# Moving two more column tiles of a layer's input from TensorE transposes to VectorE squares and a DRAM exchange, with small weights loaded later

## The reference, cut to what matters

```python
for l in range(DEPTH):
    (r_q, r_k, r_v, a_cq, a_ckv, a_kpe, l_x, l_v, l_o, l_i, l_f, c_q, z) = split(x @ w_in[l])
    ret  = head_norm(retention(r_q, r_k, r_v))
    mla  = latent_attention(rmsnorm(a_cq) @ w_uq[l], rmsnorm(a_ckv) @ w_ukv[l], a_kpe)
    mls  = head_norm(mlstm(conv(l_x) @ ml_w_q[l], conv(l_x) @ ml_w_k[l], l_v, l_i, l_f) * sigmoid(l_o)) + skip
    memo = cross_attention(c_q, mem @ w_mem_kv[l])
    y    = (concat(ret, mla, mls, memo) * silu(z)) @ w_out[l]
    x    = layernorm(ALPHA * x + y) * ln_g[l] + ln_b[l]
```

## Time and profile before

| what | value |
|---|---|
| median of 3 runs | 887.83 us (887.66 to 887.92) |
| the profiled execution | 888.09 us, of which the span of its instructions 886.3 us |
| PE busy | 880.4 us, 99% of the span |
| PEld (weight loads) | 756.2 us, 85% |
| DVE busy | 665.6 us, 75% |
| ACT busy | 488.4 us, 55% |
| TensorE clock granted | 0.999 of full speed |
| DMA | 200.33 MB, mean 226 GB/s |

### The profile page before, as it was taken

How to read it: one execution, slowest core, us unless ns; L and a number is a source line. 1 busy time by engine, 2 the same in 40 slices (tenths; PEclk the granted TensorE clock), 3 DMA queues, 4 the chain that set the end, 5 groups by cost and what they waited for, 6 DMA issues and landing times.

```text
span 886.3 us, 13162 instructions
## 1 busy us (share of the span) xinstructions
PE 880.4 (99%) x4508; PEld 756.2 (85%) x4508; DVE 665.6 (75%) x1326; ACT 488.4 (55%) x914; POOL 18.0 (2%) x18
## 2 busy tenths in 40 slices
PE   9999999999999999999999999999999999999997
PEld 8888998888888888888888889888888888888896
DVE  6869697878695677766679787968777878786765
ACT  6655776545455346544477556755355453565641
POOL 0000000000000000000000000000000001000001
PEclk9999999999999999999999999999999999999999
DMA  9796487547769677566577866884485865867832
GB/s 358 294 324 205 135 263 257 185 141 222 225 222 312 216 245 256 199 198 194 194 237 232 297 252 176 267 261 167 144 266 163 278 228 161 289 218 258 320 89 95
DMA packets 72402, 200.33 MB, mean 226 GB/s; under 512 B 9608, under 2 KB 24208, under 8 KB 71696
## 3 DMA queue, kind: packets, MB, share of 16 engines
q1 hardware_dynamic: 71760, 198.44, 67.9%
q10 hardware_dynamic: 576, 1.05, 0.4%
HBM read 183.43 MB, written 16.00 MB: 225 GB/s over the span
## 4 chain that ended last, share of the span: by engine, by line
PE 98%; issue 1%; DMA 0%; ACT 0%; POOL 0%; DVE 0%; POOLq 0%; ACTq 0%; DVEq 0%
PE acc L1357 24%; PE acc L1358 24%; PE acc L1361 24%; PE acc L1372 10%; PE acc L1378 5%; PE work L1138 1%; PE work L1137 1%; PE work L1136 1%; PE work L1262 1%; DMA B<-in_mem_t 0%; PE work L1285 0%; PE work L1274 0%; PE work L1194 0%; PE work L1188 0%; PE acc L1398 0%
## 5 line engine op out<-in xcount | busy, mean ns | idle before, releaser
L1095 ACT ACTIVATE hi<-raw 128x512 fp32r<-128x512 f32 (+2 forms) x607 | 356.3, 604 | 300.3 <-PE acc L1361 242.5
L1446 DVE TENSOR_TENSOR lo<-raw,hi 128x512 fp32r<-128x512 f32 (+2 forms) x607 | 387.2, 655 | 176.7 <-ACT hi L1095 167.8
L1357 PE MATMUL acc<-hi,xx 128*128 128x512 f32 (+2 forms) x768 | 285.5, 374 | 0.0
L1358 PE MATMUL acc<-hi,xx 128*128 128x512 f32 (+2 forms) x768 | 283.6, 372 | 0.0
L1361 PE MATMUL acc<-lo,xx 128*128 128x512 f32 (+2 forms) x768 | 223.0, 372 | 0.0
L1357 PEld LDWEIGHTS acc<-hi,xx 128*128 128x128 f32 x768 | 144.6, 188 | 23.6
L1358 PEld LDWEIGHTS acc<-hi,xx 128*128 128x128 f32 x768 | 144.6, 188 | 23.6
L1361 PEld LDWEIGHTS acc<-lo,xx 128*128 128x128 f32 x768 | 140.4, 188 | 24.6
L1372 PE MATMUL acc<-xx,hi 128*128 128x512 f32 x384 | 96.0, 392 | 0.0
L1372 PEld LDWEIGHTS acc<-xx,hi 128*128 128x128 f32 x384 | 69.3, 189 | 12.6
L1378 PEld LDWEIGHTS acc<-xx,lo 128*128 128x128 f32 x384 | 52.4, 190 | 3.7
(11 more groups left out here) (355 smaller groups left out, 960.1 us busy)
## 6 DMA issues: line engine op xcount, KB each, us to landing
raw<-in_w SPq DMA_DIRECT2D x263, 512.0 KB, 4.3
B<-turn SPq DMA_DIRECT2D x80, 128.0 KB, 4.6
raw<-in_w SPq DMA_DIRECT2D x26, 256.0 KB, 2.7
turn<-B SPq DMA_DIRECT2D x12, 512.0 KB, 5.8
raw<-in_w SPq DMA_DIRECT2D x16, 328.0 KB, 3.3
turn<-Y SPq DMA_DIRECT2D x8, 512.0 KB, 5.6
Y<-in_wuq SPq DMA_DIRECT2D x2, 1152.0 KB, 8.3
Y<-in_x_t SPq DMA_DIRECT2D x4, 512.0 KB, 8.7
```

Source lines behind the costliest of these rows:

```text
L1095: act.activation(place(l, t, hi), raw[:, s, (t % 2) * w:(t % 2 + 1) * w], ACT.Copy)\
L1357: pe.matmul(o, ah[:, q], hi[:, s, 0:w], start=k == 0, stop=False, skip_group_check=name == "memv")
L1358: pe.matmul(o, al[:, q], hi[:, s, 0:w], start=False, stop=False, skip_group_check=name == "memv")
L1446: dve.tensor_tensor(place(l, t, lo), raw[:, s, (t % 2) * w:(t % 2 + 1) * w], place(l, t, hi).bitcast(F32), ALU.subtract).then_inc(lo_done. ...
```

## The change

Layer 2's columns 512 to 1023 (`xT` 2 and 3) go the way of columns 1024 to 2047: one more pair of DVE square transposes, one more store and four more loads. The normalised blocks come in the order 1, 2, 3, 0 of column blocks, the squares behind DVE tiles 10, 12, 14, the stores at couples 10, 11, 12, the loads at couples 13, 14, 15, each waiting for its own store. The third square takes B6, so `lw` is loaded at couple 33. `wuq` is loaded at couple 36, and split behind tiles 77, 108 and 118 on ACT and 79, 109 and 120 on DVE, in both layers. `wukv` stays where it was.

```diff
-for _j in range(4):
+for _j in range(2):
     _put(LATER_PE, 18 + _j // 2 * 4, "xT", _j)
...
-    _put(LATER_ACT, 8 + _j, "normalise", (4, 5, 6, 7, 0, 1, 2, 3)[_j])
+    _put(LATER_ACT, 8 + _j, "normalise", (2, 3, 4, 5, 6, 7, 0, 1)[_j])
...
-_put(LATER_DVE, 11, "square_x", 2)
-_put(LATER_DVE, 13, "square_x", 3)
+for _cb in range(1, 4):
+    _put(LATER_DVE, 8 + 2 * _cb, "square_x", _cb)
...
 for _k in range(3):
-    _put(ACT_AT, 45 + _k, "wuq", _k)
-    _put(DVE_AT, 46 + _k, "lo", "wuq", _k)
+    _put(ACT_AT, (77, 108, 118)[_k], "wuq", _k)
+    _put(DVE_AT, (79, 109, 120)[_k], "lo", "wuq", _k)
...
-        x_squares, x_turned = ([B[i][:, 0:1024] for i in pair] for pair in ((4, 5), (2, 0)))
+        x_squares, x_turned = ([B[i][:, 0:1024] for i in pair] for pair in ((4, 5, 6), (7, 2, 0)))
...
-                    if m == 20:
+                    if m == 33:
                         sp.dma_start(B[6][:, 0:1024], a["lw"][l:l + 1, :].rearrange("o (p n) -> p (o n)", p=P))\
...
                         sp.dma_start(Y[:, 0:1024], a["wukv"][l:l + 1, :].rearrange("o (p n) -> p (o n)", p=P))\
                           .then_inc(mlaw_in.sem, 16)
+                    if m == 36:
                         sp.dma_start(Y[:, 1024:3328], a["wuq"][l:l + 1, :].rearrange("o (p n) -> p (o n)", p=P))\
...
-                    if l and m in (10, 11):
+                    if l and m in (10, 11, 12):
                         sp.wait_ge(x_squared.sem, m - 9)
-                        sp.dma_start(a["x_turn"][m - 10], x_squares[m - 10]).then_inc(x_turn_out.sem, 16)
-                    if l and m in (14, 15):
-                        sp.wait_ge(x_turn_out.sem, 2 * 16)
+                        sp.dma_start(a["x_turn"][m - 10], x_squares[m - 10]).then_inc(x_turn_out[m - 10].sem, 16)
+                    if l and m in (13, 14, 15):
+                        sp.wait_ge(x_turn_out[m - 13].sem, 16)
                         for b in range(4):
...
-                    if j < 4:
+                    if j < 2:
                         wait_job(act, l, ("xT", j))
                     else:
                         act.wait_ge(xT_in[j // 2].sem, 16 + 4 * 16)
...
-                    pe.wait_ge(normed.sem, 2 * (j // 2) + 6)
+                    pe.wait_ge(normed.sem, 2 * (j // 2) + 8)
```

More of the change, by code:

```diff
@@ L458, in build_trunk @@
         early = [Br[i][:, :].rearrange("p (a k t) -> p a k t", a=2, k=2) for i in (1, 2, 3, 0)]
-        x_squares, x_turned = ([B[i][:, 0:1024] for i in pair] for pair in ((4, 5), (2, 0)))
+        x_squares, x_turned = ([B[i][:, 0:1024] for i in pair] for pair in ((4, 5, 6), (7, 2, 0)))
         def x_block(j, n):
-            return x_turned[j // 2 - 2].rearrange("p (a i j r) -> p j i a r", a=4, i=NT, j=4)[:, j % 2 * 2 + n]
+            return x_turned[j // 2 - 1].rearrange("p (a i j r) -> p j i a r", a=4, i=NT, j=4)[:, j % 2 * 2 + n]
         def y_part(part, j):
@@ L546, in build_trunk @@
         scaled, copied = signal("scaled", 0), signal("copied", 0)
-        x_squared, x_turn_out = signal("x_squared", 0), signal("x_turn_out", 0, step=16)
+        x_squared, x_turn_out = signal("x_squared", 0), [signal(f"x_turn_out{cb}", 0, step=16) for cb in (1, 2, 3)]
         stored = signal("stored", 0, step=16)
@@ L751, in _ @@
                           .then_inc(mrow_in.sem, 16)
-                    if l and m in (10, 11):
+                    if l and m in (10, 11, 12):
                         sp.wait_ge(x_squared.sem, m - 9)
-                        sp.dma_start(a["x_turn"][m - 10], x_squares[m - 10]).then_inc(x_turn_out.sem, 16)
-                    if l and m in (14, 15):
-                        sp.wait_ge(x_turn_out.sem, 2 * 16)
+                        sp.dma_start(a["x_turn"][m - 10], x_squares[m - 10]).then_inc(x_turn_out[m - 10].sem, 16)
+                    if l and m in (13, 14, 15):
+                        sp.wait_ge(x_turn_out[m - 13].sem, 16)
                         for b in range(4):
-                            sp.dma_start(x_turned[m - 14][b * 32:(b + 1) * 32, :].rearrange("c (a n) -> c a n", a=4),
-                                         a["x_turn"][m - 14, :, b * 256:(b + 1) * 256].rearrange("(a c) n -> c a n", a=4))\
+                            sp.dma_start(x_turned[m - 13][b * 32:(b + 1) * 32, :].rearrange("c (a n) -> c a n", a=4),
+                                         a["x_turn"][m - 13, :, b * 256:(b + 1) * 256].rearrange("(a c) n -> c a n", a=4))\
                               .then_inc(xT_in[m - 12].sem, 16)
@@ L865, in normalise @@
                     blk = X[:, i, cb * 512:(cb + 1) * 512]
-                    if b == 4:
+                    if b == 2:
                         act.wait_ge(ln_done.sem, ln_done.at(l, -1))
@@ L888, in x_hi_ @@
                     for k in (2 * j, 2 * j + 1):
-                        o, f = xh[:, k, :], (bank(l, ("xT", j))[:, (k % 2) * 256:(k % 2 + 1) * 256] if j < 4 else x_block(j, k % 2))
-                        m = act.activation(o if j < 4 else o.rearrange("p (i a r) -> p i a r", i=NT, a=4), f, ACT.Identity,
+                        o, f = xh[:, k, :], (bank(l, ("xT", j))[:, (k % 2) * 256:(k % 2 + 1) * 256] if j < 2 else x_block(j, k % 2))
+                        m = act.activation(o if j < 2 else o.rearrange("p (i a r) -> p i a r", i=NT, a=4), f, ACT.Identity,
                                            scale=cols[:, C_LNG + k:C_LNG + k + 1], bias=cols[:, C_LNB + k:C_LNB + k + 1])
@@ L1498, in x_lo_ @@
                             o, f = tmp[:, (k % 2) * 256:(k % 2 + 1) * 256], \
-                                (bank(l, ("xT", j))[:, (k % 2) * 256:(k % 2 + 1) * 256] if j < 4 else x_block(j, k % 2))
-                            m = dve.tensor_scalar(o if j < 4 else o.rearrange("p (i a r) -> p i a r", i=NT, a=4), f,
+                                (bank(l, ("xT", j))[:, (k % 2) * 256:(k % 2 + 1) * 256] if j < 2 else x_block(j, k % 2))
+                            m = dve.tensor_scalar(o if j < 2 else o.rearrange("p (i a r) -> p i a r", i=NT, a=4), f,
                                                   cols[:, C_LNG + k:C_LNG + k + 1], cols[:, C_LNB + k:C_LNB + k + 1],
                                                   ALU.mult, ALU.add)
-                        if j < 4:
+                        if j < 2:
                             m.then_inc(free_bank(l, "xT", j), 1)
@@ L1513, in square_x @@
                 def square_x(cb):
-                    dve.wait_ge(normed.sem, 2 * cb - 2)
-                    to = x_squares[cb - 2].rearrange("p (b i j r) -> p i j b r", b=4, i=NT, j=4)
+                    dve.wait_ge(normed.sem, 2 * cb)
+                    to = x_squares[cb - 1].rearrange("p (b i j r) -> p i j b r", b=4, i=NT, j=4)
                     for i in range(NT):
@@ L1524, in gain @@
                         dve.wait_ge(gb0_in.sem, 16)
-                        wait_job(dve, l, ("xT", 3))
+                        wait_job(dve, l, ("xT", 1))
                     link(dve.tensor_tensor(blk, blk, gb0[:, 0, cb * 512:(cb + 1) * 512], ALU.mult))
@@ L2105 @@
     args["turn"] = nc.dram_tensor("turn", (len(TURNS), P, 4 * SEQ), F32, kind="Internal").ap()
-    args["x_turn"] = nc.dram_tensor("x_turn", (2, P, 4 * SEQ), F32, kind="Internal").ap()
+    args["x_turn"] = nc.dram_tensor("x_turn", (3, P, 4 * SEQ), F32, kind="Internal").ap()
     args["mrow"] = nc.dram_tensor("mrow", (HEADS, SEQ), F32, kind="Internal").ap()
```

## The result

The changed kernel takes 890.08 us (median of 10 runs, 888.93 to 891.64); the kernel before, on the same chip, 887.81 (887.66 to 889.17). The ratio is 1.0025, with a 95% interval from 1.0017 to 1.0034: slower by 2.27 us, where I had forecast 1.27. The runs also lie further apart than before, over 2.7 us. The profiled execution took 890.88, with a span of 889.0.

The account below looks back on a forecast made before the run. PE's own work was taken as the bound. -0.89 + 2 x 1.08 = +1.27 on the profiled 888.09 gave 889.36, and the median stands 0.26 lower: 889.1 us; own range 888.6 to 889.7, 8 in 10 from 886.9 to 891.1.

Parts of the forecast that it names:

- `wuq`'s transfer: Rival: loaded ahead of couples 37 and 38, it makes weights late, 1.0 a layer, total 891.1; chance 0.21.
- The transposes, -0.89: Layer 2, tiles 22 to 23: one pair of `xT` steps leaves PE, step 2.25 to 1.36 us, all of it showing.
- `wuq`'s first piece, 2 x 1.08: Tile 81, each layer: ACT's split 0.45 plus DVE's 0.87 late, less 0.24 margin, so PE waits 1.08 us.
- `wuq`'s pieces 2 and 3, nothing: Splits fit DVE's idle time before tiles 111 and 121; uncovered, up to 0.9 us a piece and layer.
- its transfer, nothing: `wuq` loaded at couple 36: no term in the sum; a lateness up to 1.6 us costs nothing.
- `lw`, nothing: Loaded 13 couples later, still issued thirteen tiles before it is wanted, several times a 6.5 us landing: no cost.
- "Covered": Rival: the added work is all hidden and only the transposes count, 886.9 us; chance 0.14.
- PE has reserve: Rival: PE's weight loads idle 15% of the span, so neither transposes nor waits show, 887.8 us; chance 0.05.
- The exchange of the third block, nothing: Layer 2: two DVE transposes, one store and four loads fit in idle time; uncovered transposes would cost 1.3 us.
- up to 1 us of loss: Other end of the exchange's term, `x_lo` 7 before tile 38 having the smallest margin.
- the rival made from it: Rival: the exchange comes late at tiles 34 to 38, 889.1 + 1 = 890.1 us; chance 0.05.
- The margin of 0.6 for `x_lo` 7: Layer 2, before tile 38: of 1.5 us between `x_lo` 7's end and the tile, 0.6 left as PE comes 0.89 sooner.

Follow-up runs that it names:

- e10: Kernel before with `wuq` loaded at couple 36 and split at tiles 108/109, 118/120, 122/124, two blocks exchanged, sixteen transposes: 887.78 us.
- e8: e3 without the third block's store and reload, so those features are read from a buffer with other contents: 887.37 us.
- e2: Kernel before with `wuq`'s part of the change alone (transfer at couple 36, splits at 77/79, 108/109, 118/120): 890.04 us.
- e12: e1 once more, for comparison on one chip with e9, e10 and e11: 887.43 us.
- e1: Changed kernel with `wuq`'s three pieces split in wide gaps, ACT behind tiles 108, 118, 122, DVE ahead of 109, 120, 124: 887.40 us.
- e5: e2 with DVE's split of `wuq`'s first piece moved to ahead of tile 124, ACT's split unchanged: 888.31 us.
- e7: e1 with the reloads of the three blocks at couples 13, 15, 17 instead of 13, 14, 15: 888.29 us.
- e6: e1 with `wuq`'s transfer back at couple 22: 888.71 us.
- e4: Changed kernel with `wuq`'s transfer back at couple 22, its splits still at 77/79, 108/109, 118/120: 890.54 us.
- e3: Changed kernel with `wuq` loaded at couple 22 and split at tiles 45 to 48 as before, leaving the exchange and `lw`'s move: 889.52 us.
- e9: e1 with `x_lo` 4 to 7 on DVE one or two tiles earlier, behind tiles 31, 32, 34, 35: 888.29 us.
- e11: e1 with one more 512 KB reload in the same small packets at couple 16, into a buffer nothing reads then: 889.66 us.

## Why the prediction was right, and where it was off

The forecast was for a small loss, and 890.08 is one, inside the range of 8 in 10. That it lies inside is partly luck: it is above the forecast's own range (888.6 to 889.7), and the wide one reached as far as 891.1 for the sake of `wuq`'s transfer, which costs nothing. It is also above the 889.61 up to which the prediction called the time the same, with a chance of 0.67; slower had 0.31.

*The transposes, -0.89:* right. The step from tile 22 to 23 is 1.36, and PE gains 0.89 there in every profile that lacks the transposes.

*`wuq`'s first piece, 2 x 1.08:* right in place, mechanism and parts. Measured 2.01 for both layers, and in the trace 1.06 for each; 0.21 with DVE's split gone, as its terms say.

*`wuq`'s pieces 2 and 3, nothing; its transfer, nothing; `lw`, nothing:* right, by e10 and, for `lw`, by e8. For piece 2 the reason was not: the gap before tile 111 was not used up, the tile came later instead, and PE did not need it sooner. The rival that gave the transfer 0.21 and 891.1 is out: e10 has the same transfer and no loss.

*"Covered":* out, by e2. *PE has reserve:* out, since the two waits of 1.0 at tile 81 came through as 2.01 in the time, although the weight loads are idle for 15% of the span. The rule that I had weighed there (the Trainium skill, "Perfetto Trace Analysis", section "Identifying the Most-Contended Engine") would have given no change; e2's measurement decides against reading a reserve from that share in this kernel.

*The exchange of the third block, nothing:* this is the step that failed. Without it the change is e2's 2.01 - 0.89 = 1.12 over before, and the lowest of the changed kernel's ten runs, 888.93, is just that; its median is at 2.27, so the exchange, with whatever the wait at tile 104 adds, costs about 1.15 at the median (0.54 between e10 and e12, where `wuq` is in wide gaps). Its other end, "up to 1 us of loss", was about the size, and the sign named for it, a wait at tiles 34 to 38, is what the profile shows; but the rival made from it stood at 890.1 with a chance of 0.05, which was too little. The margin of 0.6 for `x_lo` 7 was read as a fixed one. I had costed DVE's transposes, SP's time for issuing and the stores' landing, each by itself, and had put the weights of couple 14 "late by tenths at most". ACT waited 0.68, 1.24 and 0.83 for the couples 14, 15 and 16. I hadn't looked at how much of the DMA engines' time was left in that stretch: 0.97 of it was taken in the middle of it already. The mechanism that the runs show is this: with the third block the DMA engines are full for 15 us, the weights of tiles 28 to 32 land 9 to 11 us after their issue, ACT and then DVE are held up, and `x_lo` 7 or the low part of tile 37 reaches PE late. Full DMA engines alone cost nothing: in e12's profile the same three stretches have shares of 1.07, 1.07 and 1.02, and PE waits at no tile. What counts is how late the weights land. Where their median from 465 to 480 is 7.5 us or less (e1, e2, e5, e7, e8, e10, e12), PE loses nothing at tiles 37 and 38; at 8.3 it loses nothing in e6, 0.1 in e4 and 1.1 in e3; from 8.7 on (e9, the changed kernel, e11) 1.0 to 1.1. The spread of the times goes with the reloads: with two reloads the runs of an experiment lie within 0.3 to 1.3 us (e2, e5, e10, e8; the kernel before, in sets of 10 to 35 runs, within 1.5 to 3.0), with three or four within 2.4 to 6.8. That late weights are also what makes the slowest runs slow is not shown, since none of those was profiled.

What stays open: the wait at tile 104 of layer 1. It shows in the one profile of the changed kernel and in none of e2's and e4's, which have the same steps there. Layer 1 has no exchange; the weights of tile 102 landed late in that execution, for a reason that is not known. It was not tested by itself. Nor was a reload in larger packets, or by another way than through DRAM.

No version with all its transfers beats the kernel before by more than its interval: e1 is at 0.9995, from 0.9986 to 1.0003.

## What to carry to other kernels

A stage that hides a transfer must have room for it in the DMA engines' time, not only in the issuing queue and in the wanted-by time of the data: read the DMA share of the stretch first, and where it is near 1.0 before the change (0.97 here), count on the other transfers of that queue landing later, and compare that with the margin of what they feed. Work that is moved into "idle" time of an engine must be placed by how long before PE's need the next results are ready (0.24 us here at tile 81, 5.9 at tile 122), since the same 0.87 us were free in one place and cost twice 0.8 in the other. And when a median moves, look at the spread too: here a fixed wait shifted all runs alike (e2), and a contended transfer spread them (e3, e11).

## What the runs showed that was not expected

At the same full share, the DMA engines move more or less with the packets that are under way. From 460 to 465 in e1, mostly weights and stores, 545 packets carried 1.96 MB at a share of 1.00:

```profile
460.00:465.00 5.00, 5.00 (x24) 4.14 (x23) 3.53 (x7) 2.54 (x4) 0.00 (x0) 1.00 1.00 393
```

```profile
DMA packets 545, 1.96 MB, mean 393 GB/s; under 512 B 62, under 2 KB 67, under 8 KB 545
```

From 470 to 480 in the changed kernel, with the reloads under way, a share of 1.08 moved 239 and 232 GB/s. By the Trainium skill, page "DMA: Bandwidth & Descriptors", section "Specifications", 512 B is the smallest transfer for line rate; with the reloads' 1 KB runs under way the rate here was well below that of the weights and stores. Whether the size of the runs, their order in DRAM or the 32 partitions that each of the four loads writes to makes them slow was not separated. At 239 GB/s a full stretch of 5 us carries 1.2 MB instead of 1.96.
